# Alternating the order of the two matmuls of each weight tile, by k-tile

## The reference

```
for i in range(2):
    mp, ms = ada_mod(c_ctx, mod_w[i]), ada_mod(c, mod_w[i])       # 2048 -> 6*2048, one row each
    h = modulate(rms_norm(x), shift, scale)
    if i == 0: o = attention(h @ na_wqkv) @ na_wo
    else:      o = ssd_mixer(h @ ssm_w_in) @ ssm_w_out
    x = x + gate * o
    h = modulate(rms_norm(x), shift2, scale2)
    x = x + gate2 * (square(relu(h @ mlp_w1[i])) @ mlp_w2[i])
```

## Time and profile before

| what | value |
|---|---|
| time, median of 3 runs | 3034.08 us (3033.67 to 3038.32) |
| the profiled execution | 3036.24 us |
| its span, first to last instruction | 3034.4 us |
| TensorE busy | 2917.9 us (96%) |
| VectorE busy | 1723.8 us (57%) |
| ScalarE busy | 1334.7 us (44%) |
| granted TensorE clock, mean | 0.977 |
| DMA | 697.71 MB, mean 230 GB/s |

### The profile page before, as it was taken

The page is one execution under the profiler, slowest core; times in us unless marked ns, Lnnn a source line. Parts: engine busy times, 40 slices in busy tenths (PEclk is TensorE's granted clock), DMA queues, the critical chain, the costliest instruction groups (busy, mean ns, idle before and its releaser), DMA issues. The chain is left out here.

```text
span 3034.4 us, 41445 instructions
## 1 busy us (share of the span) xinstructions
PE 2917.9 (96%) x17295; PEld 2373.9 (78%) x17295; DVE 1723.8 (57%) x2471; ACT 1334.7 (44%) x1929; POOL 76.9 (3%) x94
## 2 busy tenths in 40 slices
PE   5799998999999999999989999999989999999997
PEld 2477777767777777877868888888878888888886
DVE  1344345464444445655567877777556656666665
ACT  0233335343333333433446877777443444444443
POOL 2000000000000000000000001021000000000000
PEclk7799999999999999999989999999999999999999
DMA  9888883868888888577447677675554565565652
GB/s 341 292 293 298 301 301 140 305 227 301 303 300 301 298 297 308 187 274 267 139 154 232 219 221 224 201 230 173 181 166 150 184 187 188 182 193 180 189 187 82
DMA packets 378570, 697.71 MB, mean 230 GB/s; under 512 B 12192, under 2 KB 55392, under 8 KB 377360
## 3 DMA queue, kind: packets, MB, share of 16 engines
q1 hardware_dynamic: 373568, 676.38, 65.4%
q0 software_dynamic: 4816, 18.69, 1.8%
HBM read 686.50 MB, written 8.52 MB: 229 GB/s over the span
## 5 line engine op out<-in xcount | busy, mean ns | idle before, releaser
L795 DVE TENSOR_TENSOR w_lo<-raw,w_hi 128x1024 fp32r<-128x1024 f32 x872 | 1037.1, 1220 | 971.5 <-ACT w_hi L505 971.1
L1203 PE MATMUL bank<-HL,w_hi 128*128 128x512 f32 x4368 | 1545.8, 400 | 32.8 <-DVE HL L899 30.8
L505 ACT ACTIVATE w_hi<-raw 128x1024 fp32r<-128x1024 f32 x872 | 883.9, 1048 | 1203.2 <-PE bank L1203 559.1
L1202 PE MATMUL bank<-HL,w_lo 128*128 128x256 f32 x4095 | 1166.3, 285 | 15.4 <-DVE HL L899 14.5
L1203 PEld LDWEIGHTS bank<-HL,w_hi 128*128 128x128 f32 x4368 | 811.0, 189 | 230.5 <-DVE HL L899 33.5
L1203 PE MATMUL bank<-HID,w_hi 128*128 128x512 f32 x2560 | 896.7, 397 | 0.0
L1202 PEld LDWEIGHTS bank<-HL,w_lo 128*128 128x128 f32 x4095 | 778.4, 190 | 100.9 <-issue 71.5
L1202 PE MATMUL bank<-HID,w_lo 128*128 128x256 f32 x2416 | 682.7, 283 | 0.0
L1203 PEld LDWEIGHTS bank<-HID,w_hi 128*128 128x128 f32 x2560 | 472.2, 188 | 112.3 <-issue 9.2
L1202 PEld LDWEIGHTS bank<-HID,w_lo 128*128 128x128 f32 x2416 | 456.5, 189 | 36.5 <-issue 30.2
L871 DVE TENSOR_TENSOR U<-bank,U 128x256 f32<-128x256 f32 x417 | 164.1, 420 | 168.7 <-ACT U L549 168.6
(11 more groups left out here) (201 smaller groups left out, 1292.0 us busy)
## 6 DMA issues: line engine op xcount, KB each, us to landing
raw<-in_mlp_w SPq DMA_DIRECT2D x256, 1024.0 KB, 5.5
raw<-in_mod_w SPq DMA_DIRECT2D x192, 1024.0 KB, 5.1
raw<-in_ssm_w_in SPq DMA_DIRECT2D x80, 1024.0 KB, 5.3
raw<-in_na_wqkv SPq DMA_DIRECT2D x48, 1024.0 KB, 7.2
raw<-in_ssm_w_out SPq DMA_DIRECT2D x32, 1024.0 KB, 5.0
raw<-in_na_wo SPq DMA_DIRECT2D x16, 1024.0 KB, 7.3
bc_prompt<-ac_scratch SPq DMA_DIRECT2D x16, 512.0 KB, 8.1
bc_sample<-ac_scratch SPq DMA_DIRECT2D x16, 512.0 KB, 8.4
```

The lines of the kernel that those rows point to most:

```text
L505: nc.scalar.activation(w_hi[:, k % 2, u * n:(u + 1) * n], raw[:, T % RAW_SLOTS, u * n:(u + 1) * n], ACT.Copy).then_inc(hi_ready, 1)
L795: nc.vector.tensor_tensor(w_lo[:, k % 2, s], raw[:, T % RAW_SLOTS, s], w_hi[:, k % 2, s], ALU.subtract).then_inc(lo_ready, 1)
L1202: nc.tensor.matmul(bank[b][:, 0:TOK], lo, a[:, 0:TOK], start=False, stop=False)
L1203: i = nc.tensor.matmul(bank[b][:, :], hi, a, start=first, stop=last)
```

## The change

Even k-tiles (0 and 2 of each chunk) now emit the high product first and then the low one; odd k-tiles (1 and 3) emit the low one first and then the high one, as before. The first k-tile of a group was high first already and stays so. The stream of a bank is thus high, low, low, high for each two k-tiles, where it was low, high, low, high. The number of matmuls, their operands, waits and increments stay as they are.

```
-                                if not first:
+                                if kt % 2:
                                     nc.tensor.matmul(bank[b][:, 0:TOK], lo, a[:, 0:TOK], start=False, stop=False)
                                 i = nc.tensor.matmul(bank[b][:, :], hi, a, start=first, stop=last)
-                                if first:
+                                if kt % 2 == 0:
                                     i = nc.tensor.matmul(bank[b][:, 0:TOK], lo, a[:, 0:TOK], start=False, stop=False)
```

## The result

The changed kernel takes 3015.49 us (3012.23 to 3018.01, 6 runs) against 3034.57 us (3032.83 to 3038.32) for the kernel before: a ratio of 0.9935, 95% interval 0.9923 to 0.9946. That is 19 us or 0.65% faster; the forecast was 3012 us, range 2999 to 3038.

What follows compares the result with a forecast made beforehand. The prediction took TensorE's matmul spacing as the bound, not supply. Savings of 11.6 + 2.3 + 6.4 + 1.7 = 22.0 us brought the profiled 3036.24 us to 3014.2, or 3012 us by the runs' median; range 2999 to 3038.

Steps and rivals of the forecast that it cites:

- The value of a four: Four matmuls of two neighbouring k-tiles: 0.697 us in the new order, against 0.707 in the old slow rhythm; 3047 fours change.
- The lower bound 0.693: Lowest cost taken for a new four, in us, from second-layer groups where new and old fours alternate.
- rival 2: Long runs of new fours settle in a slow rhythm, at or above 0.707 us: time 3049 us, chance 0.13.
- Groups of pattern L: 40 groups in down0_2, down0_3 and layer 1's MLP: from 22.59 to 22.30 us each, 11.6 us saved.
- wout: Output projection, 4 groups of 8 chunks, as much as 8 pattern L groups: 2.3 us saved.
- Groups of pattern LM: 40 groups with weight chunks between mod_w chunks: chunks 0 to 2 at 5.78 us, chunk 3 at 5.69; 6.4 us saved.
- mix: Scan stage, 20 groups: chunks 1 to 3 at 16.84 us, against 17.04 or 16.73 before; 1.7 us saved.
- What I put at nothing: Norms, attention, dt's stage and longer mod_w waits: no change counted, and nothing hides an earlier arrival at their edges.
- Rival 1: Order does nothing by itself; spacing belongs to the columns: time 3034 us, between 3028 and 3040, chance 0.17.
- Rival 3: In block order, a second high product in the same bank waits for the first: 74 us, time 3086, chance 0.02.
- sentence that breaks choose between the two rhythms: The old order runs at 0.707 or 0.694 us a four, and breaks in the stream choose which.
- The 325 ns a pair in either order: Estimate from the skill's spacing rule, 109 + 216 ns for low and high, making the change worth nothing.

Runs made afterwards that it cites:

- e1: Kernel before, with every k-tile high product first, then low, save the last k-tile of a group: 3037.4 us, ratio 1.0007.
- e4: Kernel before, product order kept, with all four weight chunks of groups with mod_w chunks emitted in block order: 3035.39 us, ratio 1.0001.
- e3: Kernel before, with both highs then both lows within a call and the next call turned, giving runs of four: 3027.08 us, ratio 0.9972.
- e2: Kernel before, with even k-tiles low first and odd ones high first, except a group's first and last k-tile: 3024.8 us, ratio 0.9964.
- e9: Changed kernel, with each low product cut to 128 of its 256 moving columns: 2984.68 us (one run).
- e12: Changed kernel, with each low product cut to 128 of 256 columns and 64 of 128 output features: 2817.08 us (one run).
- e5: All low products left out, so the stream is high products alone, each with its own weight load: 2483.61 us (one run).
- e7: Each k-tile emits high, low, high with the same high product twice, so lone lows stand between pairs of highs: 4646.82 us (one run).

## Why the prediction was right

**The value of a four** was the step that carried the sum. Three consecutive periods of the earlier trace rows gave 0.697, and 22.30 / 32 gives 0.697 in the changed kernel. The lower bound 0.693, read from fours standing between old ones, did not appear as the mean of a group. The old slow rhythm is 0.353 a pair and 0.707 a four over whole chunks; the "unrounded about 0.708" of the prediction, which rival 2 is priced with, is 0.001 too high.

**Groups of pattern L**: forecast 22.30 and measured 22.30. But the gain was forecast at 11.6 us and measured at 10.0. The term was mis-sized because I took the old cost, 22.59, from one group of an up phase and gave it to all. Rows of the kernel before show up1_2 and down1_2, four groups each:

```profile
2644.36 0.28 PE L1205 MATMUL bank<-HL,w_lo 128*128 128x256 f32 x1
...
2734.70 0.28 PE L1205 MATMUL bank<-HID,w_lo 128*128 128x256 f32 x1
...
2824.76 0.28 PE L1205 MATMUL bank<-HL,w_lo 128*128 128x256 f32 x1
```

90.34 and 90.06 us; the first group of down1_2 ran in the quick rhythm from chunk 1 on (5.55 us a chunk in chunks 2 and 3), the others did not. It is so in all four down phases of layer 1. There the first group also takes 22.38 in the changed kernel instead of 22.30. wout: 2.3 forecast, 2.2 measured.

**Groups of pattern LM**: 5.78, 5.78, 5.78 and 5.69 forecast, 5.78, 5.77, (5.77) and 5.69 measured; 6.4 us forecast, 6.1 measured. That the last chunk would lose 0.02 was as forecast, and so, nearly, was the first high product's 0.11 more behind each break (0.10). But that is no new cost, as rival 2 takes it to be: the old order paid it on its first low product, which starts at 939.12 in the earlier trace rows and has the next product 0.22 us behind it instead of 0.12.

**mix**: forecast 1.7, measured 3.0. The new cost was right (16.84 and 16.81). The old cost was the mean of one slow and one quick repetition; the twenty repetitions average 16.94 for chunks 1 to 3 (pauses between chunks left out), nearer the slow one, where I had 16.89. This term was mis-sized as that of pattern L was, in the other direction.

**What I put at nothing**: the gaps took 1.8 us back, nearly all in the attention, beside a longer stretch at the lower granted clock. No term of the sum had it; the prediction said that nothing hides an earlier arrival at these edges. Streams 21.3 less and gaps 1.8 more make the 19.5 of the spans. That the forecast of 22.0 came so near the 21.3 is in part luck: its errors of 1.6 and 1.3 us nearly cancel.

**Rivals.** Rival 1 fell in its general form (e1 has ratio 1.0007 and the changed kernel 0.9935: the same products with other neighbours). Its observation was right, though: lows and highs that alternate can run at 0.694 (and e1, chunk 0), so the change does not make TensorE quicker than the old order at its best; it keeps it out of the slow rhythm. Rival 2: no slow rhythm, a whole group holds 0.697. Rival 3: highs in one bank follow each other like highs in different banks, 0.23 in the chunks in block order. The prediction's sentence that breaks choose between the two rhythms stays unshown (e1, e4).

**The rule on spacing by columns.** The Trainium skill (TensorE: Matmul & The Clock Gate, section Back-to-back issue gap) gives it for isolated matmuls. The 325 ns a pair in either order, an estimate from it, was no guide here: two orders of the same products differ by 19 us.

## What to carry to other kernels

Shown for 512 and 256 columns with a weight load each. Where such long and short matmuls alternate, read the timeline from start to start, over many periods and in several phases: one stream can have two rhythms. Pair the short ones; longer runs of them don't help (e3), and a pattern broken at fixed places gives part of the gain back (e2). The paired order is the steady one, not the quickest. Take the old cost of a term as a mean over the phase, not from one group.

## What the runs showed of the hardware that I had not expected

- Alternating 512- and 256-column products have at least two stable rhythms, 0.347 and 0.353 us a pair. By the unrounded stamps of the kernel before, highs start 0.347 apart each time in the quick one, and 0.350, 0.350 and 0.360 in turn in the slow one. Neither block order (e4) nor the kind of product behind a break (e1) decides alone; what does is open.
- A product of 256 columns seems to stand at the balance between its columns and the load of the next weights: halving the columns alone moves a four from 0.697 to 0.687, halving the load alone to 0.703, halving both to 0.633. The starts of full loads are 0.11 us apart at the closest (e9). The Trainium skill (TensorE: Matmul & The Clock Gate, section LDWEIGHTS (loading the stationary operand)) gives the time of a load as its columns / 1.2 in ns, 107 ns for 128 columns. The spacing of the loads' starts in the trace agrees, and the 0.19 us that each load is recorded with doesn't. Behind a load of 64 columns the next one starts 0.06 us later (e12).
- Highs of 512 columns alone are 0.228 us apart (e5). Why not less is not settled by these runs.
- A low alone between highs can cost up to 0.010 us more by its stamp than the first of a pair (e7: 0.124, against 0.115 in the changed kernel). The runs don't explain it.
- The time at the lower clock in one stretch of the same work, the attention, differs by 3.6 us between the traces of before and after (10.4 and 6.8). The stretch is 1.6 us longer with it, nearly a tenth of the effect under test.
